# The copies that join the expert tables, moved from ACT's queue into SP's, behind the ring's loads

## What is computed

```python
idx = jnp.take_along_axis(cand_idx, pos, axis=-1)     # 8 heads x 16 experts per token
g = jax.nn.softmax(best, axis=-1)
u = expert_u[idx]
v = expert_v[idx]
act = jax.nn.gelu(jnp.einsum('td,thkd->thk', xt, u))
return jnp.einsum('thk,thkd->td', (g * act).astype(xt.dtype), v)
```

## Time and profile before

| What | Value |
|---|---|
| median of 3 runs | 1623.56 us (1617.5 to 1631.35) |
| the profiled execution, its own time | 1618.68 us |
| its span | 1616.8 us |
| PE busy / DVE busy / ACT busy | 1437.2 (89%) / 1099.1 (68%) / 785.9 us (49%) |
| moved by DMA as the queues count it | 578.23 MB, 358 GB/s over the span |
| memory read / written | 576.08 / 135.27 MB |

### The profile page before, as it was taken

The page is one execution under the profiler, slowest core; times in us unless marked ns, Lnnn a source line. Parts: engine busy times, 40 slices in busy tenths (PEclk is TensorE's granted clock), DMA queues, the critical chain, the costliest instruction groups (busy, mean ns, idle before and its releaser), DMA issues.

```text
span 1616.8 us, 24506 instructions
## 1 busy us (share of the span) xinstructions
PE 1437.2 (89%) x8308; PEld 1077.5 (67%) x8308; DVE 1099.1 (68%) x2390; ACT 785.9 (49%) x1804; POOL 271.7 (17%) x317
## 2 busy tenths in 40 slices
PE   9998999999899999998499889999977887777887
PEld 8887999998789999997499885444422232222222
DVE  6756877676568676576378668766666667666654
ACT  6646544356466344464385444444444454444433
POOL 1000010000000000000000013433333333333331
PEclk9999999999999999989699999999999999999999
DMA  9998799978996999869999859999999999999996
GB/s 322 340 366 316 267 378 385 386 286 282 359 362 226 375 385 347 277 228 335 323 348 360 312 191 380 422 421 421 421 422 421 422 420 421 422 421 421 420 422 271
DMA packets 119268, 578.23 MB, mean 358 GB/s; under 512 B 11472, under 2 KB 11616, under 8 KB 85904
## 3 DMA queue, kind: packets, MB, share of 16 engines
q0 software_dynamic: 44768, 297.78, 44.9%
q10 hardware_dynamic: 35248, 136.42, 24.7%
q1 hardware_dynamic: 39168, 142.97, 24.1%
HBM read 576.08 MB, written 135.27 MB: 440 GB/s over the span
## 4 chain that ended last, share of the span: by engine, by line
PE 48%; DMA 26%; DVE 9%; ACT 8%; issue 5%; ACTq 3%; SPq 0%; DVEq 0%; POOL 0%; POOLq 0%
DMA attn<-expert_uv,idx 12%; DMA ring<-wstream 9%; PE PS L1144 8%; PE PS L1108 7%; PE PS L620 5%; PE PS L616 5%; PE PS L611 5%; DMA late<-expert_uv,idx 5%; ACTq L1199 3%; PE PS L744 3%; PE PS L1071 2%; PE PS L642 2%; ACT wrg L1581 2%; DVE early_splits L1656 2%; PE PS L854 2%
## 5 line engine op out<-in xcount | busy, mean ns | idle before, releaser
L1656 DVE TENSOR_TENSOR early_splits<-ring,early_splits 128x1024 fp32r<-128x1024 f32 x166 | 202.2, 1221 | 76.8 <-ACT early_splits L1223 76.3
L2350 DVE CUSTOM_DVE_ANT_0 late<-late,PS 128x1024 f32<-128x1024 f32 x128 | 156.2, 1220 | 112.8 <-DMA late<-expert_uv,idx 112.8
L2350 DVE CUSTOM_DVE_ANT_0 attn<-attn,PS 128x1024 f32<-128x1024 f32 x128 | 156.1, 1220 | 97.0 <-DMA attn<-expert_uv,idx 95.6
L1223 ACT ACTIVATE early_splits<-ring 128x1024 fp32r<-128x1024 f32 x166 | 174.9, 1055 | 74.6 <-DMA ring<-wstream 43.4
L1144 PE MATMUL PS<-late,wrg 128*128 128x512 f32 x288 | 145.4, 630 | 43.4 <-ACT wrg L1581 43.4
L1573 ACT ACTIVATE gel<-dot 128x1 f32<-128x1 f32 x256 | 51.2, 200 | 266.8 <-DVE dot L2350 266.6
L1144 PE MATMUL PS<-attn,wrg 128*128 128x512 f32 x288 | 142.3, 619 | 31.7 <-ACT wrg L1581 31.2
L558 POOL DMA_INDIRECT attn<-expert_uv,idx x128 | 121.3, 948 | 248.1 <-PE PS L1144 103.1
L558 POOL DMA_INDIRECT late<-expert_uv,idx x128 | 119.9, 936 | 231.9 <-PE PS L1144 116.9
L1144 PEld LDWEIGHTS PS<-late,wrg 128*128 128x128 f32 x288 | 49.9, 191 | 135.5 <-ACT wrg L1581 98.1
L1144 PEld LDWEIGHTS PS<-attn,wrg 128*128 128x128 f32 x288 | 50.7, 193 | 123.3 <-ACT wrg L1581 80.9
(11 more groups left out here) (412 smaller groups left out, 3008.9 us busy)
## 6 DMA issues: line engine op xcount, KB each, us to landing
ring<-wstream SPq DMA_DIRECT2D x258, 512.0 KB, 9.8
expert_uv<-expert_u ACTq DMA_DIRECT2D x64, 1024.0 KB, 20.0
expert_uv<-expert_v ACTq DMA_DIRECT2D x64, 1024.0 KB, 20.8
ada<-w_ada POOLq DMA_DIRECT2D x32, 512.0 KB, 9.6
late<-w_ada POOLq DMA_DIRECT2D x16, 512.0 KB, 8.9
late<-wstream SPq DMA_DIRECT2D x4, 512.0 KB, 11.1
attn<-expert_uv,idx POOLq DMA_INDIRECT x128, 15.2
late<-expert_uv,idx POOLq DMA_INDIRECT x128
```

Of the source, the lines that this page charges most:

```text
L1223: act.activation(hi_of(u), raw(u), ACT.Copy).then_inc(hi_ready, 1)
L1656: ve.tensor_tensor(lo_of(u), raw(u), hi_of(u).bitcast(F32), ALU.subtract).then_inc(units_begun, 1)
L2350: ve.tensor_tensor_reduce(row, row, H2N[n // 8], 1.0, 0.0, ALU.mult, ALU.add, dot[:, n % 2, k:k + 1]).then_inc(dot_ready, 1)
```

## The change

Each copy has 128 rows in place of 256, so there are 256 of them. All calls of `join_rows` on ACT go away. SP issues the copies: in the projection stages and in the third stage, behind the load of each unit from number 6 on, one copy for an even unit and two for an odd one, up to unit 249; in the feed-forward loop, behind four of the six loads of each turn, in all 11 turns. The two tables count on separate semaphores, and POOL waits for both.

```diff
-JOIN_ROWS = 256
+JOIN_ROWS = 128
 JOINS = 2 * 128 * 128 // JOIN_ROWS
+LOOPED = 4
...
+            joined = [0]
+
+            def join_rows(count, i=None):
+
+                for c in range(joined[0], joined[0] + count):
+                    table, half, done = ((expert_u, slice(0, D), u_joined), (expert_v, slice(D, 2 * D), v_joined))[c % 2]
+                    at = c // 2 * JOIN_ROWS
+                    rows = slice(at, at + JOIN_ROWS) if i is None else bass.ds(i * (LOOPED // 2 * JOIN_ROWS) + at, JOIN_ROWS)
+                    sp.dma_start(expert_uv[rows, half], table[rows, :]).then_inc(done, 16)
+                joined[0] += count
...
                     load(u, order[u])
+                    if u >= RING:
+                        join_rows(1 + u % 2)
                 at += PROJ_UNITS[layer]
+                assert joined[0] % 2 == 0
                 with sp.Fori(0, 3 * NF // RING) as i:
                     for m in range(RING):
                         sp.wait_ge(units_begun, i * RING + (at + m - RING + 1))
                         load(at + m, at + m, i)
+                        if m % 3 < 2:
+                            join_rows(1, i)
+                joined[0] += LOOPED * (3 * NF // RING - 1)
...
                 load(u, order[u + SIDE] if u >= SPLIT_UNITS else order[u])
-
+                if u < WO2_AT + RING:
+                    join_rows(1 + u % 2)
+
+            assert joined[0] == JOINS
...
-                    gp.wait_ge(tables_joined, 16 * JOINS)
+                    gp.wait_ge(u_joined, 8 * JOINS)
+                    gp.wait_ge(v_joined, 8 * JOINS)
...
-            joined = [0]
-
-            def join_rows(i=None, m=0):
-
-                c = joined[0] if i is None else m
-                table, half = ((expert_u, slice(0, D)), (expert_v, slice(D, 2 * D)))[c % 2]
...
-                act.dma_start(expert_uv[rows, half], table[rows, :]).then_inc(tables_joined, 16)
...
                     split_hi(FUSED_AT[layer] + s + 2)
-                    join_rows()
-                    if s % 5 == 0:
-                        join_rows()
...
-                    if c < HELD - 1:
-                        join_rows()
...
                         split_hi(u + 3 * m + 1, i)
-                        join_rows(i=i, m=m)
                         split_hi(u + 3 * m + 2, i)
-                joined[0] += NF - 4
...
                 split_hi(LX_AT + c + 2)
-                join_rows()
...
                 split_hi(GATE2_AT + c + 2)
-                join_rows()
-                join_rows()
...
                 split_hi(MERGE_AT + c + 2)
-                join_rows()
```

More of the change, by code:

```diff
@@ L383, in two_blocks @@
         query_landed = [sem(f"query_landed{k}") for k in range(SIDE // 2)]
-        tables_joined = sem("tables_joined")
+        u_joined, v_joined = sem("u_joined"), sem("v_joined")
         row_landed = [sem(f"row_landed{k}") for k in range(SLOTS)]
@@ L1538, in _ @@
             act.activation(RECH[:, KC - 1, :], XC[:, KC - 1, :], ACT.Copy).then_inc(rech_ready, 1)
-            assert joined[0] == JOINS
             for j in range(4):
```

## The result

The changed kernel takes 1551.76 us (median of 4 runs, 1550.31 to 1554.07) against 1621.7 us before; the ratio is 0.9577, with a 95% interval from 0.9542 to 0.9612. The direction was right, the size wasn't.

The account below looks back on a forecast made before the run. Before the first indirect load, PE and the DMA engines were seen near their limits, with ACT held by its full copy queue. Gains of 47.5 us less 5.5 gave 42, so 1576.7, set at 1579 us; 8-in-10 range 1556 to 1612.

Parts of the forecast that it names:

- (A): Projection stage of layer 0, 80 to 140 us: PE loses 8.5 us to ACT's held issues, to be won back.
- (B): Layer 1, 400 to 475 us: PE is busy 65.8 of 75 us, so 9.2 us to be won back.
- (C): Gate steps and recurrence, 750 to 802 us: 31 us lost, less 5 for ACT's own work, so 26 to win.
- (D): One more held issue on the chain, at 873 us: 3.9 us to be won.
- (E): Units 232 to 243: copies delay loads, PE stands 11 us where it stood 5.6, so 5.5 us given back.
- The feed-forward loops: Each turn moves the same 6.8 MB, 18.2 us at 373 GB/s against PE's 17.3: no change, with 5 us either way.
- The check by bytes: Before the first indirect load, 291 MB must pass in 838 us, at 347 GB/s: possible, with little left, limiting the gain.
- The half copy at the price of half a whole: A 128-row copy costs the DMA engines 1.54 us, taken from the whole copies' queue share; no row shows one alone.
- SP's issues at nothing: SP's 256 added issues, at most 1.4 us per unit with two copies, against units 2.9 us or more apart, cost nothing.
- R3: Rival, more than forecast: small issues count too (11 us) and the loops' loads land in time (7 us); 1561 us, chance 0.13.
- R2: Rival, slower: copies and ring loads in one queue hold each other up in loops and projections; 1663 us, chance 0.11.
- R1: Rival: the DMA engines can't follow, and ACT's wait becomes one for ring loads; 1612 us, chance 0.16.

Follow-up runs that it names:

- e1: The kernel before, with each 256-row copy of ACT issued as two copies of 128 rows at the same place; 1622.29 us, ratio 0.9996.
- e11: The changed kernel with its 128-row copies, issued by SP, bunched over the units as in the kernel before; 1577.15 us, ratio 0.9737.
- e3: The changed kernel with its 128-row copies issued by ACT on its own queue, behind each unit's rounding, as many per unit; 1551.87 us, ratio 0.9577.
- e9: Against the changed kernel: 256-row copies issued by ACT, evenly spread, three behind four units and one per three units in the loops; 1564.18 us, ratio 0.9668.
- e2: The changed kernel with copies of 256 rows, issued by SP behind three loads of four, two per loop turn; 1561.69 us, ratio 0.9632.
- e7: The changed kernel with copies moved out of the output stretch to earlier units, none from unit 232 on; 1542.5 us, ratio 0.9536.
- e10: The changed kernel with copies of 64 rows, twice as many behind each load; 1551.2 us, ratio 0.9591.

## Why the prediction fell short, step by step

The medians, between the places of the copies and their issuer, all with halves:

| | ACT issues | SP issues |
|---|---|---|
| places of before | 1622.3 (e1) | 1577.2 (e11) |
| even | 1551.9 (e3) | 1551.8 (changed) |

*What bounds it, and that ACT's held issues cost most: right, but half of the story.* The bunching fills a queue. If that is ACT's queue, it costs 70 us; if SP's, 25. Either edit, issuer or spread, ends the held issues on ACT; only the spread also ends what they stood for. The spread alone, with wholes on ACT's queue as before, brings e9 from 1620 to 1564 us. I had named the bunching (5.1 us of DMA per unit against 4.3 on PE) and priced it only by ACT's stops.

*(A) and (B), 8.5 and 9.2 us:* measured 9.7 and 12.4. Right in place, but ending ACT's stops does not win (A): e11, in which ACT is not held, still has a first stage of 163.4 us. (B) was low: I took PE's idle time and left out that for a part of the time it also worked at the lower clock (0.93 in 400:475, where the changed kernel has 1.00 in 383:450).

*(C), 26 us:* measured 33.2 over the gates. The term was undersized. The 5 us left for ACT's own work need not have been: the changed kernel has the same table loads in gates of 48.6 us. The window also ended at 802, while the last gate matmuls came at 808.67.

*(D), 3.9 us:* measured 0.2 in the merge, as the stretch up to the recurrence's output is as long without the held issue. On the chain of before, the split behind that issue releases SP, and among the loads that SP then issues is the one that takes 21.78 us to land:

```profile
877.83 1.05 ACT early_splits L1223
...
880.79 1.15 DVE early_splits L1656
...
881.95 0.33 SPq L476
```

So its 3.9 us run into the output stretch, where (E) is. The two were forecast at -1.6 us together and measured at -1.3. That the one hid in the other is read from the chain; no run tries it.

*The feed-forward loops, "I count 0": the step that failed, 13.8 us in all.* I divided the bytes of a turn by 373 GB/s, got 18.2 us against 17.3 on PE, took the loop to be bound by the DMA engines and wrote "this balance stays as it is". But 373 was what the loop moved, not what the engines can move: the changed kernel moves 388 in that loop, at PE's pace, e2 moves 381 with wholes, also at PE's pace, and 418 stood in my own rows for ring loads (885:895). A share of 0.99 did not mean that nothing more would go through. PE's losses came from single loads that landed late beside whole copies in ACT's queue; ACT waited up to 3.1 us for one, 31 us in all. e9 still has 19 us of these waits, and all of the 4.8 us, in the first loop; the changed kernel has none of either. For the second, which is 9.0 us shorter, e1 wins 5.1 of it by smaller pieces alone and e9 has 7.7 of it with wholes; I can't divide that one cleanly.

*(E), 5.5 us given back:* measured 1.5. The place was right. Free of copies the stretch takes 47.7 us (e7, e11), so PE lost 9.0 there in the changed kernel (forecast 11) and 7.5 before (I had 5.6). A unit with its copies needs less than my 3.74 us: 1.31 MB at the 390 GB/s of that stretch are 3.4, which makes the deficit 12 x 0.48 = 5.8 us instead of 10.3.

In all: 67.7 us came where 42 were added up. Of the 25.7 more, the loops have 13.8, (C) 7.2, (B) 3.2, (A) 1.2, and (D) and (E) together 0.3.

*The check by bytes, which kept me from forecasting more:* failed for the same reason as the loops. 347 GB/s looked like the edge of what 325 to 373 allow; the changed kernel has 352 in the mean over 30:844 at a share of 0.95. The rates of stretches filled with whole copies were no ceiling for halves.

*The half copy at the price of half a whole, 1.54 us:* somewhat high for the one queue. SP's queue, loads and copies together, took 48.7% of 1548.6 us for 277.2 MB, 2.72 us for a million bytes, so 1.43 for 0.524 MB in the mean of both; before, loads took as much, copies 2.93 for a million. Where halves have ACT's queue almost for themselves (e3, 25.3% of 1548.4 us for 136.43 MB) they took 2.87, which is 1.51 each and near my price.

*SP's issues at nothing, the rows' stage unchanged, the copies done before the first indices:* right, as far as the runs show. SPq has 1% of the chain now, but e3, in which SP issues no copy, is no faster. POOL's first indirect load comes at 887.46 (forecast some 913), and it waited for indices, not for copies.

*The rivals.* R3 had the right sign and was sized at 18 us over the forecast where 27 came. Its first reason falls: e3 makes all 256 small issues on ACT and pays nothing for them. Its second came true, at 13.8 us where it had 7: the loops' loads land in time. But that is not for want of a third queue, since e3 has three and the same first loop. R2 is refuted: one mixed queue is no slower (e3 against the changed kernel). R1 happened where I had not put it, in e11.

*The Trainium skill* ("DMA: Bandwidth & Descriptors", section "Rules for kernel authors") holds that spreading DMAs over issuing engines brings no bandwidth; e3 against the changed kernel, 1551.87 and 1551.76 us, agrees. The same section's 1 MiB or more per DMA for full bandwidth is not what these runs show: beside ring loads, in one queue, the stretch from 30 to 80 us moved 385 GB/s with 512 KB copies and 345 with 1 MB copies. The measurement decides for this mixture. The fixed part of about 2 us per DMA, which the prediction looks for in the section "Bandwidth", stands in the section "Anatomy of one DMA — SWDGE (gpsimd) path", for DMAs that GpSimd issues. No such price shows here: 128 more copies cost nothing (e1 against before), nor did 256 more (e10 against the changed kernel).

## What to carry to other kernels

Background transfers should be given out at a constant number of bytes per unit of foreground work, since a crowd of them costs twice: by the loads that come late, and by every instruction that is queued behind an issue that is held back; if they can't be even, they belong on an engine that has nothing else to do. Leave the stretch free of them in which the foreground itself lives on its loads. A DMA share near 1 next to a busy PE need not be a ceiling, it was 0.99 at 373 GB/s here and 1.00 at 388 after the change: compare the rate with the highest that any stretch reaches before you divide by it.

## What the runs showed of the hardware that I had not expected

Copies from memory to memory in pieces of 512 KB, in one queue with 512 KB loads, took 11% less of the DMA engines' time per byte than pieces of 1 MB: a share of 1.01 at 385 GB/s against 1.02 at 345, from 30 to 80 us. Pieces of 256 KB gave the same as 512 KB (1.01 at 384). On ACT's queue, with the places of before, the smaller pieces gave nothing (0.97 at 325 against 0.98 at 332). With an even spread there, they took 4% less from 30 to 80 us (e3, 0.92 at 311, against e9, 0.97 at 316) and 9% less from 815 to 870 (1.03 at 416 against 1.02 at 376). Loads and copies are not mixed in the same proportion in all these stretches, so the figures are of the mixtures. I have not found out why.
